# Two-layer decoder trunk in fp32 on one core: the three norms over all features run over two halves of the tokens

## The reference

```python
for layer in range(2):
    h = rms_norm(r, norm_mix_pre[layer])
    proj = h @ w_in[layer]                 # latents, q, k, v, gates
    ...                                    # two attention branches, gated sum
    mix = (sigmoid(g_a) * out_a + sigmoid(g_b) * out_b) @ w_out[layer]
    r = r + rms_norm(mix, norm_mix_post[layer])
    h = rms_norm(r, norm_ffn_pre[layer])
    gu = h @ w_gate_up[layer]
    ff = (silu(gu[..., :D_FF]) * gu[..., D_FF:]) @ w_down[layer]
    r = r + rms_norm(ff, norm_ffn_post[layer])
return r[:, 16:272, :]

def rms_norm(x, gain):
    return x * rsqrt(mean(x * x, axis=-1) + 1e-6) * gain
```

## Time and profile before

| | us |
|---|---|
| median of 3 runs | 835.7 (835.64 to 836.18) |
| the profiled execution | 835.84 |
| its span in the profile | 834.0 |
| PE busy | 819.4 (98%), 6453 matmuls |
| DVE busy | 595.4 (71%) |
| ACT busy | 451.9 (54%) |
| POOL busy | 123.4 (15%) |
| mean granted TensorE clock | 0.997 |

### The profile page before, as it was taken

How to read it: one execution, slowest core, us unless ns; L and a number is a source line. 1 busy time by engine, 2 the same in 40 slices (tenths; PEclk the granted TensorE clock), 3 DMA queues, 4 the chain that set the end, 5 groups by cost and what they waited for, 6 DMA issues and landing times.

```text
span 834.0 us, 17173 instructions
## 1 busy us (share of the span) xinstructions
PE 819.4 (98%) x6453; PEld 792.6 (95%) x6453; DVE 595.4 (71%) x1000; ACT 451.9 (54%) x749; POOL 123.4 (15%) x125
## 2 busy tenths in 40 slices
PE   8999999999999999999999999999999999999997
PEld 8998999999999999999999999899999999999885
DVE  4999586669597666666668995876787976766432
ACT  6755555475565444455556546554765654554431
POOL 2122000004331111101112220000053111111000
PEclk9999999999999999999999999999999999999999
DMA  8656422235526545445552555222363565565631
GB/s 280 224 189 205 148 77 102 76 103 181 173 88 217 180 172 177 131 139 185 178 199 86 200 195 185 95 101 99 108 224 103 182 219 182 177 194 172 207 104 50
DMA packets 38744, 131.55 MB, mean 158 GB/s; under 512 B 4384, under 2 KB 4768, under 8 KB 38688
## 3 DMA queue, kind: packets, MB, share of 16 engines
q1 hardware_dynamic: 38688, 130.77, 47.0%
HBM read 129.70 MB, written 1.05 MB: 157 GB/s over the span
## 4 chain that ended last, share of the span: by engine, by line
PE 84%; DVE 12%; issue 2%; ACT 1%; DMA 1%; SPq 0%; DVEq 0%; POOL 0%; POOLq 0%
PE bank L1110 21%; PE bank L1112 20%; PE bank L1111 20%; DVE w_lo L700 3%; PE bank L1140 3%; PE bank L1462 2%; PE bank L1463 2%; PE bank L1461 2%; PE bank L1335 2%; PE bank L1311 2%; PE bank L1159 2%; PE bank L1144 1%; DVE h_lo L722 1%; PE bank L1350 1%; DVE resid L737 1%
## 5 line engine op out<-in xcount | busy, mean ns | idle before, releaser
L700 DVE TENSOR_TENSOR w_lo<-w_raw,w_hi 128x1024 fp32r<-128x1024 f32 x250 | 336.0, 1346 | 39.2 <-ACT w_hi L344 37.1
L1110 PE MATMUL bank<-h_hi,w_hi 128*128 128x272 f32 (+1 forms) x1232 | 357.6, 290 | 2.1 <-DVE dv_t L718 0.9
L1112 PE MATMUL bank<-h_hi,w_lo 128*128 128x272 f32 (+1 forms) x1232 | 352.1, 286 | 0.0
L1111 PE MATMUL bank<-h_lo,w_hi 128*128 128x272 f32 (+1 forms) x1232 | 351.3, 285 | 0.0
L344 ACT ACTIVATE w_hi<-w_raw 128x1024 fp32r<-128x1024 f32 x250 | 262.6, 1054 | 127.7 <-PE bank L1112 54.7
L1110 PEld LDWEIGHTS bank<-h_hi,w_hi 128*128 128x128 f32 x1232 | 232.0, 188 | 4.2 <-issue 1.3
L1112 PEld LDWEIGHTS bank<-h_hi,w_lo 128*128 128x128 f32 x1232 | 231.9, 188 | 0.0
L1111 PEld LDWEIGHTS bank<-h_lo,w_hi 128*128 128x128 f32 x1232 | 231.6, 188 | 0.0
L624 POOL TENSOR_TENSOR acc<-acc,sq 128x272 f32<-128x272 f32 (+1 forms) x48 | 48.5, 1011 | 148.2 <-ACT sq L357 147.6
L669 POOL TENSOR_TENSOR pbuf<-sbuf,ubuf 128x272 f32<-128x272 f32 (+1 forms) x44 | 37.4, 850 | 210.2 <-DVE ubuf L1048 207.2
L1048 DVE TENSOR_TENSOR ubuf<-bank,rstd_h 128x272 f32<-128x272 f32 (+1 forms) x44 | 19.0, 431 | 48.1 <-PE bank L1112 48.0
(11 more groups left out here) (209 smaller groups left out, 1250.6 us busy)
## 6 DMA issues: line engine op xcount, KB each, us to landing
w_raw<-weights SPq DMA_DIRECT2D x220, 512.0 KB, 4.0
w_raw<-weights SPq DMA_DIRECT2D x16, 384.0 KB, 3.0
w_raw<-weights SPq DMA_DIRECT2D x16, 320.0 KB, 2.8
resid<-x_t SPq DMA_DIRECT2D x4, 272.0 KB, 5.4
out_tokens<-o_tok SPq DMA_DIRECT2D x4, 256.0 KB, 2.0
cst<-consts SPq DMA_DIRECT2D x1, 544.0 KB, 4.9
gain_bc<-gain_rows SPq DMA_DIRECT2D x1, 512.0 KB, 6.7
y<-consts SPq DMA_DIRECT2D x1, 256.0 KB, 5.3
```

Source lines behind the costliest of these rows:

```text
L700: dve.tensor_tensor(w_lo[:, n % RING, :], w_raw[:, n % RAW, :], w_hi[:, n % RING, :].bitcast(f32), ALU.subtract).then_inc(lo_ready, 1)
L1110: pe.matmul(dst, wh, hi, start=first, stop=False)
L1111: pe.matmul(dst, wh, lo, start=False, stop=False)
L1112: return pe.matmul(dst, wl, hi, start=False, stop=last)
```

## The change

At the three boundaries the tokens are split at column 144: half A is columns t0 to 143 (144 wide, or 128 where t0 is 16), half B columns 144 to 271 (128 wide).

- The last tiles of the stage (out: tiles 5, 6 and 7; down: tile 7) run first for half A into their own banks, then again with the same weights for half B into banks 4, 5 and 6 (`half_tile`). The sums of squares of half A and the spread of its factor stand inside half B's tiles.
- The first four tiles of the next stage run as two passes over the 8 chunks, half A, then half B (`half_pass`). The post-norm of half B and the pre-norms of both halves have their sums and spreads inside these passes.
- `keep_clock` of 10 and 28 matmuls is gone at the three boundaries.
- DVE, ACT and POOL do all their work of a boundary per half. DVE's residual loop alternates between two buffers (`tres`, `rstd_q`), makes the product of chunk c before it adds chunk c-1, and makes h_lo of chunk c-2.
- Norm events are counted per half (`E(K, h)`), the squares that PE adds itself get buffers of their own (`last_sq`), and one split of weights (w_lo) moves past the end of the boundary.

```diff
+WHOLE, A, B = "whole", "A", "B"
+MID = 144
+GROUP = {"out": (5, 6, 7), "down": (7,)}
+LATE = {"out": {0: 5, 2: 6, 4: 7}, "down": {3: 7}}
+BANK_B = {5: 4, 6: 5, 7: 6}
+POST_BANK, PRE_BANK = {A: 7, B: 4}, {A: 7, B: 5}
...
             def boundary(b, l, st, K, gp, later):        # DVE
...
+                for m in GROUP[st]:
+                    to_y_half(K, l, st, m, A)
+                recip(E(K, A), len(chunks_of(A, t0)))
+                residual(b, l, st, K, A, gp)
+                split(later)
+                residual(b, l, st, K, B, gp)
+                take(E(K + 1, A), PRE_BANK[A], rstd_h, *columns(A, t0))
+                recip(E(K + 1, B), len(chunks_of(B, t0)))
+                take(E(K + 1, B), PRE_BANK[B], rstd_h, *columns(B, t0))
...
+            def half_tile(l, st, m, src, h, hooks={}):   # PE
...
+                        pe.matmul(dst, wh, src[k][0][:, a:e], start=k == 0, stop=False)
+                        pe.matmul(dst, wh, src[k][1][:, a:e], start=False, stop=False)
+                        mm = pe.matmul(dst, wl, src[k][0][:, a:e], start=False, stop=k == len(src) - 1)
...
+            def boundary(b, l, st, K, tiles):            # PE
...
+                half_pass(b, l, st, tiles, A, {2: sums_b, 4: lambda: norm_spread(K, POST_BANK[B], t0, B)})
+                half_pass(b, l, st, tiles, B, {1: lambda: norm_sums(K + 1, PRE_BANK[A], t0, A), 5: lambda: norm_spread(K + 1, PRE_BANK[A], t0, A),
+                                               KC - 1: lambda: norm_sums(K + 1, PRE_BANK[B], t0, B)}, lambda: norm_spread(K + 1, PRE_BANK[B], t0, B))
...
-            def post_norm(K):
-
-                norm_sums(K, 7, t0)
-                keep_clock(10)
-                norm_spread(K, 7, t0)
-                keep_clock(28)
...
-                post_norm(K0 + POST_MIX)
+                for m in GROUP["out"]:
+                    half_tile(l, "out", m, mixed, A)
+                half_tile(l, "out", 5, mixed, B, {3: lambda: norm_sums(K0 + POST_MIX, 7, t0, A)})
+                half_tile(l, "out", 6, mixed, B, {0: lambda: norm_spread(K0 + POST_MIX, 7, t0, A)})
+                half_tile(l, "out", 7, mixed, B)
```

More of the change, by code:

```diff
@@ L128, in __init__ @@
         self.slots = len(self.slot_done)
-        self.sq0, self.add0, self.sq_place, self.sq_free = {}, {}, {}, {}
-        s = a = 0
-        users = []
-        for l in range(DEPTH):
[L135 to L145, removed]
+        squares = [(PRE_MIX, c, WHOLE) for c in range(KC)]
@@ L148, in build_trunk @@
+        for K, h in norms:
+            if K % NORMS != NDIFF:
+                mine = [self.add_at[n] for n in users if n[0] == K and n[2] in (h, WHOLE)]
+                self.adds[K, h] = max(mine) + 1
+        self.half_before, n = {}, 0
+        for l in range(DEPTH):
+            for st in ("out", "down"):
+                self.half_before[l, st] = n
+                n += len(GROUP[st])
 def build_trunk(nc: bass.Bass, xT, weights, gains, lam_in, consts, gain_rows, out):
@@ L376, in _ @@
+                root(E(K + 1, B), PRE_BANK[B], D_MODEL, len(chunks_of(B, t0)))
+                for n in later[1:]:
+                    split(n)
             act.wait_ge(const_ready, 1)
@@ L594, in _ @@
                         square_tile(K0 + POST_FFN, TD + m, m)
-                    root(K0 + POST_FFN, 7, D_MODEL, t0)
-                    boundary(2 * l + 2, K0 + NORMS + PRE_MIX, G_MIXPRE, l + 1)
+                    split(SD + 4 * (KC - 1) + HI_AHEAD)
+                    boundary(2 * l + 2, l, "down", K0 + POST_FFN, G_MIXPRE, l + 1, [SD + 4 * (KC - 1) + j + HI_AHEAD for j in range(1, 4)])
             split(SD + HI_AHEAD)
@@ L1152, in sums @@
+            def sums(chunks, bank, col, srcs, count=True, last_ready=None):
                 for s, src in enumerate(srcs):
@@ L1218, in _ @@
                 else:
-                    first_tiles([(TL("lat") + q, S("lat") + q, *((late, t0) if q < QC else (full, 0))) for q in range(BANKS)],
-                                (h_hi, h_lo, KC * 2 * l), {KC - 1: lambda: norm_sums(K0 + PRE_MIX, 7, 0)},
-                                lambda: norm_spread(K0 + PRE_MIX, 7, 0))
+                    boundary(2 * l, l - 1, "down", K0 - NORMS + POST_FFN,
+                             [(TL("lat") + q, S("lat") + q, t0 if q < QC else 0) for q in range(BANKS)])
                 for i in range(4, 6):
```

419 lines of the change are left out of this document (287 added, 132 removed).

## The result

The changed kernel takes 910.25 us, the median of four runs (909.94 to 912.20), against 835.94 (835.64 to 836.26) for the kernel before on the same chip: a ratio of 1.0895, 95% interval 1.0883 to 1.0908. It is slower, as forecast, by 74.3 us where 44.3 were forecast.

A forecast was written before the change was run, and what follows sets the result against it. PE, busy 98% of the span, was taken to bound the kernel. Boundaries at +13.8, +15.3 and +14.7 us plus 0.5 for DVE gave 44.3 on top of 835.84, so 880 us; range 855 to 915.

The forecast's parts named there:

- the forecast's main term: At the boundaries, 498 matmuls become 996, each paced by its weight load: 0.222 us a split matmul instead of 0.126.
- a clock that falls for a part: Lower TensorE clock during part of the half-width work; with a half matmul costing 0.14, the reason for stretching to 915.
- a load that hides: Half-width matmuls at the boundaries hide their loads, 0.072 or 0.065 us each: 827 to about 840 us; chance 5%.
- the plain fp32 rate: Narrow fp32r matmuls at the boundaries run like plain fp32, 0.24 and 0.21 us each: 986 us; chance 10%.
- what was costed at nothing on DVE: Inside the boundaries, DVE's doubled steps and pipelined residual loop are hidden by PE's own work: no gain or cost.
- the three sums: PE time forecast for the boundaries: 42.3, 43.0 and 41.1 us, against 28.5, 27.7 and 26.4 before.
- the 2 us that PE was to wait for the first chunk of half B: Second boundary: DVE starts late with only one tile split ahead, so PE waits 2 us (0 to 4).
- the 0.15 for each place where sums or spreads are put in: Eight places a boundary, 0.15 us each by the idle time around 227.78, 1.2 us in all.
- The 0.5 us put on DVE behind the second boundary: Two weight splits behind the first latent tile delay lat_lo and the next bank's release: 0.5 us (0 to 2.5).
- the second rival: At the boundaries TensorE gets the lower clock: 958 to 990 us, some 910 if for a third; chance 4%.
- worth nothing: At the boundaries, the pipelined residual loop and the removal of the identity matmuls change the time by nothing.
- a prize of 4 us a boundary: Filler and waiting at a boundary, 38 identity matmuls included, that the change could save: 4 us, some 12 in all.

The follow-up runs named there:

- the first experiment: Kernel before plus 240 fp32r matmuls, 24 each at ten widths from 512 to 32 columns, inside out tile 2 of layer 0; 868.61 us, one run.
- the fourth experiment: Kernel before with the same 498 matmuls issued as two halves, in the old order, norms unsplit, identity matmuls kept; 888.79 us, ratio 1.0636.
- the seventh experiment: Changed kernel with sums over accumulated squares in fp32r against two columns of ones, one record a chunk instead of two, 30 fewer; 875.52 us, ratio 1.0483.
- experiments 5: Kernel before plus 480 fp32r matmuls of 128 columns in one row inside out tile 2 of layer 0; 888.67 us, one run.
- experiment 6: Kernel before plus ten times 44 matmuls of 128 columns followed by eight one-column records; 937.62 us, one run.
- 3: Changed kernel with bf16 matmuls against zeros spread evenly, one a chunk in half tiles, four in half passes; 895.09 us, ratio 1.0712.
- 2: Changed kernel with eight bf16 matmuls against zeros behind nearly every place of sums or spreads at the boundaries; 883.62 us, ratio 1.0611.
- experiment 8: Changed kernel with only tile 7 of the out projections split, tiles 5 and 6 at full width; 920.21 to 939.79 us, ratio 1.1016.
- 9: Changed kernel without the product h_hi * w_lo in the half-width matmuls, 664 instead of 996; 875.44 us, ratio 1.0492.
- experiment 7: Changed kernel with accumulated squares summed in fp32r, one record a chunk instead of two, the last tile's squares left in fp32; 875.52 us, ratio 1.0483.

## Why the prediction was right, and where it was wrong

**How it was right.** The direction, the range of 855 to 915 and the forecast's main term came out. The range held 910 only because it had been stretched for "a clock that falls for a part", a case with a chance of 4%; the forecast's own range, 871 to 892, was missed. So the mechanism on record explains some 40 of the 74 us, and that the rest still fell inside is luck.

**Right: direction, and the term that decides it.** A half-width matmul costs its weight load, 0.111 us, at 144 columns as at 128 (timeline after; the first experiment down to 64). The two bounds, 0.072 for a load that hides and 0.24 for the plain fp32 rate, are both out. The Trainium skill, page "TensorE: Matmul & The Clock Gate", section "Back-to-back issue gap", has 81 ns for a load and matmul pair at 128 columns; with fp32 loads 111 was measured, and the measurement decides. That the halves by themselves carry the loss is shown by the fourth experiment, and with the clock at 1.00 the seventh puts the whole change at +39.8 us, and up to 3.3 more for its missing records, against a forecast of 44.3.

**Right: what was costed at nothing on DVE.** The pipelined loop is worth nothing (ratio 0.9996), and PE waits for no chunk of h_hi or h_lo. DVE is busy 20 of the 40 us of a boundary at full clock.

**Small terms: too high inside the boundaries, too low behind one.** With the clock at 1.00 the forecast for the seventh experiment's kernel would be the three sums less its missing records there: 42.3, 43.0 and 41.1 less 0.7, 0.7 and 0.4. Measured: 40.7, 39.5 and 39.8. So I had 0.9, 2.8 and 0.9 us too much. In the second it is the 2 us that PE was to wait for the first chunk of half B, which does not exist, since DVE keeps ahead; the rest fits the 0.15 for each place where sums or spreads are put in. That 0.15 was misread: at 227.78 it is a wait for h_hi, not the price of a place. In the timeline after, the eight records of the first sums take 222.79 to 223.65, 0.86 us, which is their loads and no more. The 0.5 us put on DVE behind the second boundary was too low: from there to the start of the third PE is busy 174.21 of 175.80 us in the kernel before, and 174.42 of 177.60 in that of the seventh experiment, with five records fewer, so it is about 2 us.

**Wrong: the clock.** The step that failed is the sentence against the second rival: "around the one-column sums at 223.5 the clock stayed at 1.00". It did, but 38 identity matmuls stood beside those sums, and the change takes them away. The same prediction called them "worth nothing". The experiment without fillers (the eleventh) shows that the clock falls there even in the kernel before, though PE idles there too; with full-width tiles behind, it is back after 3.4 us in the run profiled, and the whole costs 3.3 us. The fourth experiment shows the difference in one kernel, without idling: at its first two boundaries the twelve records with identity matmuls behind them leave the clock at 1.00, and the twelve without are followed by the fall. The changed kernel has half-width tiles behind, and with those it does not come back. I had the rows for this and did not set them side by side. The rival had 4%, and its own price ("some 910 if it is for a third") is close to what came: half clock in 15.4 of 48.1 and 53.1 of 64.7 us of the boundaries.

The account of the 74.3 us: 39.8 is the change at full clock (seventh experiment, with 30 records fewer), up to 3.3 are those records, and at least 31 the clock. From the trace of after itself: the first boundary is 48.1 where 40.7 + 0.7 are needed at full clock, 6.7 us; the second 64.7 where 39.5 + 0.7 are, 24.5; behind each of them some 5 us of full-width tiles run at half clock, about 2 each. Together 35. The two ways agree within 4 us. The 2 us behind the second do not reach the end: from there to the start of the third boundary the changed kernel takes 177.5 us and that of the seventh experiment 177.6.

**What is shown and what is not.** Shown: the one-column records between half-width matmuls start the fall (experiments 5 and 6, alike but for them, one run each); fillers beside them prevent it (3, and 2 in three runs of four; within one kernel, 4), and so does a quarter of the records less (7); half-width work with a place of sums every 11 to 19 us does not end it (after, 6). Not run: a fall followed by half-width work without any sums. Open: why it started behind the eight records at 243.5 and not behind the eight at 222.8 (it fell at 246.5), and why not at the third boundary, which has four at a place; in experiments 8 and 9 the clock fell at the third boundary as well, with four at a place. In every one of these kernels the falls come 1 to 6 us behind the start of a place of sums, but not each such place makes one. Whether it is the number of records, their nearness or their plain fp32 form was not separated: experiment 7 changes all three a little.

## What to carry to other kernels

Before a matmul is split along its moving side, look at what a weight load alone takes between two one-column matmuls: a split that goes below that costs the whole load again, whatever it lets overlap, and a prize of 4 us a boundary can't pay for 168 loads more. Idle-time fillers on TensorE are part of the schedule: when a change removes them, ask what stood beside them, what follows (here the clock came back behind full-width work alone), and how long it would stay low. And when a kernel's runs begin to spread by a per cent, read the clock's row first, since it can hide a gain (experiment 8) or nearly double a loss (39.8 to 74.3 us here). Runs that agree do not clear it, though: the changed kernel's four lie within 0.3%, and all four had the low clock.

## What the runs showed of the hardware

- An fp32r matmul follows the last by 0.227 us at 512 columns and 0.12 at 256, and never by less than 0.108 to 0.111, down to 32 columns: the 128-column weight load of fp32 sets that floor.
- At granted clock 0.50 the floor is 0.21 us at 128 columns, 1.9 times the 0.111 at 1.00.
- A clock that has fallen stays low through 53 us (second boundary after) and 87 us (experiment 6) of half-width work with sums in between and PE busy all the time, while 53.6 us of half-width work that began at 1.00 stayed at 1.00. Half-width matmuls can run at either level; which one went with the one-column records between them.
- Eight bf16 matmuls of 128 columns take 0.41 us and, put behind each place of sums, kept 1.00 in the run profiled; one of the four runs had a mean of 0.984.
- Twelve one-column records between half-width matmuls left the clock at 1.00 where 38 bf16 matmuls stood behind them, and it was at 0.50 within 1.4 us of the start of twelve such records without them (experiment 4).
